# A two-block transformer on one core: the residual products' PSUM banks are emptied by ScalarE into SBUF, and VectorE adds from there

## The reference, cut to what matters

```python
# first block, layer l
h = h + mixer(rms_norm(h, attn_norm[l]), ...)          # ... ends in  o @ w_out
h = h + conv_glu_ffn(rms_norm(h, ffn_norm[l]), ...)    # ... ends in  (silu(conv) * up) @ w_down
# second block, layer l
h = layer_norm(DN_ALPHA * h + mix, ln1_g[l], ln1_b[l]) # mix = y @ w_out
h = layer_norm(DN_ALPHA * h + conv_ffn(h, ...), ln2_g[l], ln2_b[l])
```

## Time and profile before

| what | value |
|---|---|
| median of 3 runs | 2911.27 us (2907.41 to 2917.86) |
| profiled execution, own time | 2911.27 us |
| its span | 2909.3 us |
| PE busy | 2715.9 us, 93% of the span |
| DVE busy | 1731.0 us, 59% |
| ACT busy | 1049.0 us, 36% |
| POOL busy | 1024.8 us, 35% |
| mean granted TensorE clock | 0.961 |
| L626, the residual additions | 96 instructions, 66.0 us |
| L435, the high parts of weights | 363 instructions, 404.4 us |
| L409, the low parts of weights | 363 instructions, 982.0 us |

### The profile page before, as it was taken

The page is one execution under the profiler, slowest core; times in us unless marked ns, Lnnn a source line. Parts: engine busy times, 40 slices in busy tenths (PEclk is TensorE's granted clock), DMA queues, the critical chain, the costliest instruction groups (busy, mean ns, idle before and its releaser), DMA issues.

```text
span 2909.3 us, 34536 instructions
## 1 busy us (share of the span) xinstructions
PE 2715.9 (93%) x11434; PEld 2000.5 (69%) x11434; DVE 1731.0 (59%) x2256; ACT 1049.0 (36%) x1586; POOL 1024.8 (35%) x385
## 2 busy tenths in 40 slices
PE   6999999999998999999698988999989898899997
PEld 5654688887764578888375456788767644587875
DVE  4645775486386577287559336827634944583672
ACT  2344322223144342232443544323335345432333
POOL 2211244444321234444144113444424421244452
PEclk9998999999999899999899999999999999999999
DMA  3110123232211123232111011232311110122221
GB/s 135 66 44 30 58 94 106 90 99 89 87 51 37 36 94 98 90 101 97 43 51 58 29 36 61 92 100 94 100 62 58 51 37 29 65 92 96 94 98 68
DMA packets 56069, 212.16 MB, mean 73 GB/s; under 512 B 6192, under 2 KB 6448, under 8 KB 55856
## 3 DMA queue, kind: packets, MB, share of 16 engines
q1 hardware_dynamic: 55120, 209.60, 21.7%
q10 hardware_dynamic: 864, 1.44, 0.2%
HBM read 208.92 MB, written 2.10 MB: 73 GB/s over the span
## 4 chain that ended last, share of the span: by engine, by line
PE 71%; DVE 12%; ACT 7%; issue 5%; POOL 4%; DVEq 1%; DMA 0%; ACTq 0%; POOLq 0%
PE bank_G L462 19%; PE bank_G L464 19%; PE bank_G L463 19%; PE bank_S L1080 4%; POOL wlo L409 3%; DVE conv_up L711 2%; PE bank_O L1090 2%; PE bank_X L1100 2%; DVE mx L1973 1%; PE bank_S L509 1%; ACT whi L435 1%; DVE prod L731 1%; PE bank_X L1645 1%; DVE scores_t L1623 1%; PE bank_X L780 1%
## 5 line engine op out<-in xcount | busy, mean ns | idle before, releaser
L409 POOL TENSOR_TENSOR wlo<-raw,whi 128x1024 fp32r<-128x1024 f32 (+1 forms) x363 | 982.0, 2706 | 1754.0 <-ACT whi L435 1754.0
L462 PE MATMUL bank_G<-n_hi,whi 128*128 128x512 f32 x2392 | 976.1, 408 | 61.6 <-DVE n_lo L566 28.6
L464 PE MATMUL bank_G<-n_hi,wlo 128*128 128x512 f32 x2392 | 944.2, 395 | 0.0
L463 PE MATMUL bank_G<-n_lo,whi 128*128 128x512 f32 x2392 | 944.1, 395 | 0.0
L435 ACT ACTIVATE whi<-raw 128x1024 fp32r<-128x1024 f32 (+1 forms) x363 | 404.4, 1114 | 841.7 <-PE bank_G L464 826.5
L462 PEld LDWEIGHTS bank_G<-n_hi,whi 128*128 128x128 f32 x2392 | 457.4, 191 | 204.4 <-issue 64.1
L464 PEld LDWEIGHTS bank_G<-n_hi,wlo 128*128 128x128 f32 x2392 | 456.3, 191 | 99.2
L463 PEld LDWEIGHTS bank_G<-n_lo,whi 128*128 128x128 f32 x2392 | 457.5, 191 | 95.5 <-issue 7.7
L626 DVE SCALAR_TENSOR_TENSOR h<-h,bank_G 128x512 f32 (+1 forms) x96 | 66.0, 688 | 392.2 <-PE bank_G L464 392.2
L462 PE MATMUL bank_G<-a_hi,whi 128*128 128x512 f32 x704 | 275.3, 391 | 5.6 <-DVE a_lo L733 3.7
L463 PE MATMUL bank_G<-a_lo,whi 128*128 128x512 f32 x704 | 274.0, 389 | 0.0
(11 more groups left out here) (279 smaller groups left out, 2604.2 us busy)
## 6 DMA issues: line engine op xcount, KB each, us to landing
raw<-in_w_mix_in SPq DMA_DIRECT2D x42, 512.0 KB, 3.3
raw<-in_w_out SPq DMA_DIRECT2D x32, 512.0 KB, 3.3
raw<-in_w_hyb_in SPq DMA_DIRECT2D x25, 512.0 KB, 3.3
raw<-in_w_diff_in SPq DMA_DIRECT2D x24, 512.0 KB, 3.2
raw<-in_w_up0a SPq DMA_DIRECT2D x22, 512.0 KB, 3.3
raw<-in_w_up0b SPq DMA_DIRECT2D x22, 512.0 KB, 3.3
raw<-in_w_up1a SPq DMA_DIRECT2D x22, 512.0 KB, 3.2
raw<-in_w_up1b SPq DMA_DIRECT2D x22, 512.0 KB, 3.3
```

The source lines that it names most:

```text
L409: pool.tensor_tensor(b.wlo[:, g.slot, 0:width], b.raw[:, g.slot, 0:width], b.whi[:, g.slot, 0:width], ALU.subtract).then_inc(b.lo_ready, 1)
L462: pe.matmul(out, b.whi[:, g.slot, w], hi[:, k, :], start=(k == 0), stop=False)
L463: pe.matmul(out, b.whi[:, g.slot, w], lo[:, k, :], start=False, stop=False)
L464: mm = pe.matmul(out, b.wlo[:, g.slot, w], hi[:, k, :], start=False, stop=(k == pieces - 1))
```

## The change

In all 12 residual groups ACT now empties the bank: `take` copies `bank_G` to `b.mixed[g % 2]`, increments `evacuated`, and then makes `whi` of tile g+2 as before. DVE waits for `evacuated` and adds from `b.mixed`; it increments a new semaphore `resid_done`. ACT waits for `resid_done` of tile g-2 before it writes the slot again. `RES` gives each group its first count of `resid_done`. Waits on `evacuated` whose purpose was that `h` is added now go to `resid_done`; in `out0` and `out1` the eight `gained_hi_act` wait each for their own tile instead of all for the last. Two waits of ACT at the start of the up and mixer products (`act.wait_ge(b.evacuated, g0)`) are gone, since ACT has emptied the bank before itself. 96 instructions are added on ACT, none is removed on any engine; on DVE the 96 additions read SBUF instead of PSUM.

```diff
-def products_act(act, b, name, gain=None):
+def products_act(act, b, name, r0, gain=None):
     g0, tiles = group_tiles(name)
     width = WIDTH[g0]
     if gain:
         for k in range(tiles):
-            split_hi(act, b, Index(g0 + k + 2))
+            wait(act, b.resid_done, r0 + k - 1 if k else max(r0 - 1, 0))
+            take(act, b, Index(g0 + k), b.mixed[:, (g0 + k) % 2, :])
             if k and not name.startswith("out"):
-                act.wait_ge(b.evacuated, g0 + k)
+                act.wait_ge(b.resid_done, r0 + k)
                 gained_hi_act(act, b, gain, k - 1)

         for k in range(0 if name.startswith("out") else tiles - 1, tiles):
-            act.wait_ge(b.evacuated, g0 + (tiles if name.startswith("out") else k + 1))
+            act.wait_ge(b.resid_done, r0 + k + 1)
             gained_hi_act(act, b, gain, k)
         return

-    for i, g, g_next in pairs(act, g0, tiles - 2):
-        split_hi(act, b, g.after(2), width)
-        split_hi(act, b, g_next.after(2), width)
-    split_hi(act, b, Index(g0 + tiles))
-    split_hi(act, b, Index(g0 + tiles + 1))
+    def one(g, r, w=None):
+        wait(act, b.resid_done, r)
+        take(act, b, g, b.mixed[:, g.slot, :], width=w)
+
+    one(Index(g0), max(r0 - 1, 0))
+    one(Index(g0 + 1), r0)
+    for i, g, g_next in pairs(act, g0 + 2, tiles - 4):
+        one(g, r0 + 1 + 2 * i, width)
+        one(g_next, r0 + 2 + 2 * i, width)
+    one(Index(g0 + tiles - 2), r0 + tiles - 3)
+    one(Index(g0 + tiles - 1), r0 + tiles - 2)
...
-    def one(g, h, last=False):
-        dve.wait_ge(b.gemm_done, g.at(1))
-        dve.scalar_tensor_tensor(h, h, float(alpha), b.G[:, g.slot, :], ALU.mult, ALU.add).then_inc(b.evacuated, 1)
+    def one(g, h, r, last=False):
+        dve.wait_ge(b.evacuated, g.at(1))
+        ins = dve.scalar_tensor_tensor(h, h, float(alpha), b.mixed[:, g.slot, :], ALU.mult, ALU.add).then_inc(b.resid_done, 1)
         if stats == "square":
-            dve.wait_ge(b.evacuated, g.at(1))
+            dve.wait_ge(b.resid_done, r)
             link(dve.tensor_tensor(b.sq[:, 0, :], h, h, ALU.mult))
...
+RES = {}
+for _n in range(4):
+    RES.update({f"out{_n}": 24 * _n, f"down{_n}a": 24 * _n + 8, f"down{_n}b": 24 * _n + 16})
...
-    if not scaled:
-        act.wait_ge(b.evacuated, g0)
     chunk(Index(g0), Index(g0 + 1), c0, 0, W8, W8)
```

More of the change, by code:

```diff
@@ L301, in allocate @@
     b.nlo_ready = sem("nlo_ready")
+    b.resid_done = sem("resid_done")
     b.conv_done = sem("conv_done")
@@ L641, in products_dve @@
                 dve.sem_inc(b.acc_ready, 1)
-            one(Index(g0 + k), b.h[:, k, :], last=k == tiles - 1)
+            one(Index(g0 + k), b.h[:, k, :], RES[name] + k + 1, last=k == tiles - 1)
             if k and not name.startswith("out"):
@@ L651, in products_dve @@
         for s, x in enumerate((g, g_next)):
-            one(x, b.h[:, bass.ds(2 * i + s, 1), :].rearrange("p a t -> p (a t)"))
+            one(x, b.h[:, bass.ds(2 * i + s, 1), :].rearrange("p a t -> p (a t)"), RES[name] + 1 + s + 2 * i)
     link.end(looped // 2)
     if stats:
-        one(Index(g0 + tiles - 2), b.h[:, tiles - 2, :])
+        one(Index(g0 + tiles - 2), b.h[:, tiles - 2, :], RES[name] + tiles - 1)
         dve.sem_inc(b.acc_ready, 1)
-        one(Index(g0 + tiles - 1), b.h[:, tiles - 1, :], last=True)
+        one(Index(g0 + tiles - 1), b.h[:, tiles - 1, :], RES[name] + tiles, last=True)
+RES = {}
+for _n in range(4):
+    RES.update({f"out{_n}": 24 * _n, f"down{_n}a": 24 * _n + 8, f"down{_n}b": 24 * _n + 16})
 def ffn_up_pe(pe, b, name, nlo):
@@ L747, in ffn_act @@
         ffn_up_act(act, b, f"up{f}{tag}", FC * f + HC * half)
-        products_act(act, b, f"down{f}{tag}", gain if half else None)
+        products_act(act, b, f"down{f}{tag}", RES[f"down{f}{tag}"], gain if half else None)
 def ffn_dve(dve, b, link, f, stats, gain=None, nhi=0):
@@ L2180, in _ @@
             hyb_attention_act(act, b)
-            products_act(act, b, "out0", "ffn_norm0")
+            products_act(act, b, "out0", RES["out0"], "ffn_norm0")
             rms_scale_act(act, b, link, 1)
@@ L2187, in _ @@
             diff_attention_act(act, b, link)
-            products_act(act, b, "out1", "ffn_norm1")
+            products_act(act, b, "out1", RES["out1"], "ffn_norm1")
             rms_scale_act(act, b, link, 3)
@@ L2196, in _ @@
                 mixer_act(act, b, link, l, mixw)
-                products_act(act, b, f"out{2 + l}")
+                products_act(act, b, f"out{2 + l}", RES[f"out{2 + l}"])
                 layer_norm_act(act, b, link, 6 + 2 * l, f"ln1_b{l}", 64 + 24 * l, True)
```

## The result

The changed kernel takes 2930.87 us (median of 6 runs, 2922.97 to 2939.97), the kernel before 2911.20 us beside it (6 runs, 2907.41 to 2917.86): ratio 1.0068, 95% interval 1.0046 to 1.0091. It is slower by 0.68%, about 20 us, where 6.3 us were forecast. The profiled execution after took 2924.7 us (span 2922.2), 13.4 us more than the profiled one of before, with a mean granted clock of 0.957 against 0.961.

A forecast was written before the change was run, and what follows sets the result against it. PE, busy 93% of the span, was taken to set the pace, with copies inside groups hidden. Ends of 4.85 us and starts of 1.47 us gave 6.3 us on 2911.27 us: 2917.6 us, 0.22% slower, range 2909 to 2926 us.

The forecast's parts named there:

- the lower bound: DVE's addition from SBUF: bounds of 0.69 and 0.75 us for the instruction, 0.69 kept.
- rival 3: At group ends the last `sq` falls behind POOL and ends 2.46 us later: 2923.9 us in all; chance 0.18.
- Relief: PE's waits for `wlo`, mostly outside the groups, fall by over 15 us: at most 2892.6 us; chance 0.07.
- late splits: Inside groups, without the 1.2 us of slack, every split comes late, 96 x 0.49 = 47 us: 2958 us; chance 0.03.
- Ends: Eight group ends at a norm: 0.49 us each at five, 0.80 each at `down0b`, `down1b`, `down3b`; 4.85 us.
- Starts: Third gemms of `out1`, `out2`, `out3` wait for `wlo`, 0.49 us later each: 1.47 us; elsewhere covered.
- rival 1: At the norms, clock drops worth 1.6 us each shift; two fewer 2914.4 us, two more 2920.8; chance 0.12.
- The prediction's own sign: A difference to before in stretches that hold no residual group would be the clock.

The follow-up runs named there:

- refill_after: Changed kernel with three small unused constant matmuls on PE ahead of every norm's last sum: 2925.08 us, ratio 1.0049 to the kernel before.
- out1_last: Kernel before with one copy, only the last tile of `out1` going over ACT: 2916.80 us beside 2912.99, ratio 1.0014.
- shift4_before: Kernel before with 4 small constant matmuls (0.9 us) ahead of the last sum of `down2b` alone: 2910.66 us, ratio 0.9979.

## Why the prediction was wrong

**Right.** The direction and the chain. Nothing inside the groups behind their starts, but for 0.36 us at the last tile of `out0` and 0.18 us at the seventh of `out2` and `out3`: `whi` is 0.49 us later, all down groups are within 0.13 us. The addition at 0.69 us at the ends, on the lower bound; the mean of 0.73 comes from three of the 96, of 1.44 to 2.77 us, that met POOL's splits. The rule of the Trainium skill's Vector Engine (DVE) Microarchitecture Reference, "Points that are easy to get wrong", that two such SBUF sources halve the rate, stays contradicted: 0.69 us here against 686 to 692 ns from PSUM. The last `sq` did not fall behind POOL (rival 3), by 0.34 us. Relief and late splits (rivals 2 and 4) did not come either: PE waits 25.1 us for `wlo`, before 25.0.

**Ends, forecast 4.85 us.** Measured from the last tile's emptying: `out0` +0.64, `out1` +0.64, `down0b` +0.63, `down1b` +0.64, `down3b` +0.64, and the end of the first subtraction in `out2`, `out3` and `down2b` +0.43 each: 4.48 us. The addition was 0.63 later and not 0.80; in `out0` and `out1` the path moved by more than the 0.49, since POOL's split queued behind `sq` (2.57 for 2.35).

**Starts, forecast 1.47 us.** The four out groups, first to last tile, grew by 0.42, 0.75, 0.83 and 0.79: 2.8 us. Up to the third tile it is 0.06, 0.68, 0.65 and 0.61, so `out0` was rightly taken for free at its start and the others cost 0.6 to 0.7 instead of 0.49. The 0.36 at the last tile of `out0` are a copy that starts 0.55 us behind PE's next matmul, where in `out1` it is 0.26; why stays open. PE's waits at the third gemms are 2.12, 1.91 and 1.87 us, forecast 1.2, 1.7 and 1.7. In `out1` the clock rose to 2.4 GHz 1.6 us earlier, so PE was through with the gemm ahead sooner and waited for the same `wlo` for longer. The start of `out2` after:

```profile
1721.06 0.60 ACT L443 ACTIVATE mixed<-bank_G 128x512 f32<-128x512 f32 x1 [1.88 <-PE bank_G L466]
1721.55 1.05 ACT L437 ACTIVATE whi<-raw 128x1024 fp32r<-128x1024 f32 x1
1721.81 0.69 DVE L634 SCALAR_TENSOR_TENSOR h<-h,mixed 128x512 f32 x1 [1.36 <-ACT mixed L443]
1722.54 0.69 DVE L644 TENSOR_TENSOR acc<-acc,h 128x512 f32<-128x512 f32 x1
1722.77 5.50 POOL L411 TENSOR_TENSOR wlo<-raw,whi 128x1024 fp32r<-128x1024 f32 x2 [58.25 <-ACT whi L437]
...
1725.59 0.49 PE L464 MATMUL bank_G<-n_hi,whi 128*128 128x512 f32 x1 [1.91 <-POOL wlo L411]
```

DVE's `acc` starts 0.23 us ahead of POOL and ends at 1723.23, 0.46 us behind POOL's start; before, POOL met 0.32 us of it. PE's wait is 1.91 us, before 1.20: 0.49 for `whi`, 0.14 for the longer overlap with `acc`, and 0.08 that I can't place. The sum of both terms is 7.3 us against 6.3: a size off, not the reason for the miss.

**The step that failed** is the term for the clock, which the sum has at nothing: rival 1, "the clock at the norms", with its sentence against a sign, "nothing in the change picks one". Its price per drop was right. From the last tile of `out2` to the next product's first matmul it took 18.68 us and now takes 20.62, 0.43 direct and 1.5 of clock; `down2b` (20.30) and `out3` (20.35) had that drop before. With the last layer norm, 2.14 us longer with 0.64 direct, this makes two more drops at layer norms, 3.0 us, close to the 3.2 of the rival's upper bound. But I read the shift as neutral for the clock, though the sum itself said that PE idles longer at the norms, and the clock went down in every set of runs with late last tiles but that with long fillers. I had also bounded it by two layer norms, while a drop reaches into the dense product behind: behind `out1` it costs 2.7 us alone. And the interleaving in the second mixer, 4.8 us beyond its direct delay, stood in the prediction as relief only (rival 2), with no price on the slow side.

Of the roughly 16 to 20 us by the two ratios, 7.3 are direct and 9 to 13 are not. That rest is in part matmuls at 1.2 GHz, 8.9 us more of PE's busy time in the five stretches of the one profile, and in part idleness that I can't place. The prediction's own sign came true: a difference in stretches that hold no residual group.

**What is shown, and what isn't.** Shown: the slowdown, twice; that eight late last tiles carry the larger part of it and lower the mean granted clock (0.9568 over 12 runs against 0.9604 over 35), and that fillers raise it again; that the direct delays are 7.3 us by the timeline. Argued: that the lower clock is what costs the rest. The profiles put it at 2.7 us behind `out1` and 1.5 us at each of two layer norms; refill_after gives back only 2 us by the ratios and 6 by the medians. Open: what decides whether 3 us of idleness end in a drop (out1_last had none), what the second mixer's +5 hangs on, why refill_after kept +1.9 behind `out2` and +2.1 at the end, and how much of it a mean over many profiles would leave.

## What to carry to other kernels

A hop added to a chain that another engine's work covers costs nothing, whatever its number; on a serial chain between dense matmul stretches it costs its latency and, beyond that, what a lower TensorE clock and a shifted interleaving take: here the whole was more than twice the latency. So empty the bank by the extra hop only where nothing waits for the sum, and add the last tile of a group directly. Where PE idles at norms, matmuls on constants in the gap can pay for themselves: 2906.0 us against 2910.3 here (ratio 0.9980, 0.9968 to 0.9991), without any other change.

## What was not expected of the hardware

- The granted clock is sensitive to 0.7 us. In the kernel with 0.7 us more of idleness at each of eight norms (1.0 at the first) the mean clock went from 0.961 to 0.957 and 0.952 in two profiles: from about 227 us at 1.2 GHz (2 x 0.039 x 2909) to 251 and 282. Fillers raised it to 0.971. The Trainium skill, TensorE: Matmul & The Clock Gate, Part 1, says that the gate's watch runs freely, so that the same kernel shows another number of slow matmuls from run to run; the runs agree, with the 7.5 us by which an untouched stretch differed in shift4_before, and with the +1.01 and +8.50 us of one stretch in two profiles of the changed kernel.
- The exclusion of POOL and DVE works in POOL's disfavour too: a `wlo` that comes 0.35 to 0.41 us before the end of DVE's `sq` takes 2.57 and 2.66 us instead of 2.35 and 2.46, where it came 0.14 and 0.21 us before that end: the length grew by about the overlap that was added.
- ACT's copy out of PSUM (0.60 us) releases DVE 0.63 us behind its start at the group ends and up to 0.76 us behind it at other tiles, and ACT's own next instruction 0.49 us behind it.
